# Retention's and attention's small steps placed on other tiles: value tile before root, last head one tile up, attention's products one tile back

## The reference, cut to what matters

```python
proj = h @ w_in                                   # block 1: q, k, v, g_ret, u, two gates
q = rope(q); k = rope(k) * 128 ** -0.5            # 8 heads of 128, v of 256 columns
scores = (q @ k.T) * decay ; inner = scores @ v   # causal, decay ** distance
ret = head_group_norm(inner + cross)              # (y - mean) * rsqrt(var + eps) per token
y_ret = (silu(g_ret) * ret) @ w_ret_out
y_s5 = ...                                        # 64 groups, complex diagonal scan, gelu, GLU
merged = sigmoid(gate_r) * y_ret + sigmoid(gate_s) * y_s5
x = x + gt_m * rmsnorm(merged @ w_out) ; x = x + gt_f * rmsnorm(ffn(x))
# block 2, one block of 256 keys: attention is causal softmax with ALiBi
p = softmax(q @ k.T * scale - slope * distance) ; o_a = p @ v
```

## Time and profile before

| | us |
|---|---|
| median of three runs (3452.05 to 3454.35) | 3454.16 |
| the profiled execution | 3456.49 |
| its span on the core | 3454.6 |
| PE busy | 3298.0 (95%) |
| DVE busy | 2389.5 (69%) |
| ACT busy | 1494.9 (43%) |

### The profile page before, as it was taken

How to read it: one execution, slowest core, us unless ns; L and a number is a source line. 1 busy time by engine, 2 the same in 40 slices (tenths; PEclk the granted TensorE clock), 3 DMA queues, 4 the chain that set the end, 5 groups by cost and what they waited for, 6 DMA issues and landing times.

```text
span 3454.6 us, 53480 instructions
## 1 busy us (share of the span) xinstructions
PE 3298.0 (95%) x20912; PEld 2990.6 (87%) x20912; DVE 2389.5 (69%) x2467; ACT 1494.9 (43%) x1538; POOL 445.8 (13%) x309
## 2 busy tenths in 40 slices
PE   1799999999989999999989999999999999999998
PEld 0799999999978888888868888888888888888887
DVE  8799987787676666655676667657767766666554
ACT  1455555544444344433354344344344444434332
POOL 2065556720100000000000000000002100000000
PEclk7899999999999999999999999999999999999999
DMA  9665554568745555567734444555555555555554
GB/s 399 269 235 219 217 206 173 187 246 302 300 151 184 194 186 190 190 233 258 266 111 167 171 159 175 191 182 190 193 183 198 185 190 187 193 185 190 190 190 146
DMA packets 111026, 706.34 MB, mean 204 GB/s; under 512 B 13376, under 2 KB 24256, under 8 KB 30672
## 3 DMA queue, kind: packets, MB, share of 16 engines
q1 hardware_dynamic: 100416, 693.86, 54.8%
q10 hardware_dynamic: 10512, 11.11, 1.0%
HBM read 702.83 MB, written 2.10 MB: 204 GB/s over the span
## 4 chain that ended last, share of the span: by engine, by line
PE 82%; DVE 8%; issue 4%; ACT 3%; POOL 2%; DMA 2%; DVEq 0%; ACTq 0%; POOLq 0%; SPq 0%
PE acc L523 44%; PE acc L524 23%; PE acc L520 4%; PE acc L521 4%; PE acc L522 4%; DVE ring_lo L1307 2%; ACT ring_hi L859 1%; DMA ring_raw<-w_ada 1%; DVE ring_raw L1329 1%; POOL s_w L1985 1%; PE p_norm L569 1%; POOL s_x L1987 0%; DVE aside_y L1329 0%; PE p_y L587 0%; POOL s_x L1984 0%
## 5 line engine op out<-in xcount | busy, mean ns | idle before, releaser
L1307 DVE TENSOR_TENSOR ring_lo<-ring_raw,ring_hi 128x2048 fp32r<-128x2048 f32 (+1 forms) x576 | 1312.4, 2280 | 571.8 <-ACT ring_hi L859 570.3
L523 PE MATMUL acc<-h_split,ring_hi 128*128 128x512 f32 x4736 | 1655.5, 392 | 9.2 <-DVE h_split L1369 4.5
L524 PE MATMUL acc<-h_split,ring_lo 128*128 128x256 f32 x4736 | 1337.5, 282 | 0.0
L859 ACT ACTIVATE ring_hi<-ring_raw 128x2048 fp32r<-128x2048 f32 (+1 forms) x576 | 1070.8, 1862 | 414.4 <-DMA ring_raw<-w_down 152.0
L523 PEld LDWEIGHTS acc<-h_split,ring_hi 128*128 128x128 f32 x4736 | 891.7, 188 | 197.3 <-issue 9.7
L524 PEld LDWEIGHTS acc<-h_split,ring_lo 128*128 128x128 f32 x4736 | 897.7, 190 | 0.4
L523 PE MATMUL acc<-ffn_split,ring_hi 128*128 128x512 f32 x1408 | 488.2, 390 | 0.0
L520 PE MATMUL acc<-h_split,ring_hi 128*128 128x256 f32 x1408 | 403.7, 287 | 82.9 <-DVE h_split L1369 69.8
L1926 POOL TENSOR_TENSOR sq_sum<-sq_sum,tile 128x256 f32<-128x256 f32 x60 | 76.6, 1277 | 2568.9 <-ACT tile L885 2568.9
L524 PE MATMUL acc<-ffn_split,ring_lo 128*128 128x256 f32 x1408 | 397.1, 282 | 0.0
L521 PE MATMUL acc<-h_split,ring_hi 128*128 128x256 f32 x1408 | 396.3, 281 | 0.0
(11 more groups left out here) (342 smaller groups left out, 3814.2 us busy)
## 6 DMA issues: line engine op xcount, KB each, us to landing
ring_raw<-w_ff SPq DMA_DIRECT2D x88, 1024.0 KB, 4.8
ring_raw<-w_down SPq DMA_DIRECT2D x64, 1024.0 KB, 4.8
ring_raw<-w_ffb SPq DMA_DIRECT2D x56, 1024.0 KB, 4.8
ring_raw<-w_heads SPq DMA_DIRECT2D x48, 1024.0 KB, 4.8
ring_raw<-w_mix SPq DMA_DIRECT2D x48, 1024.0 KB, 4.8
ring_raw<-w_ada SPq DMA_DIRECT2D x32, 1024.0 KB, 7.4
ring_raw<-w_ret SPq DMA_DIRECT2D x32, 1024.0 KB, 4.8
ring_raw<-w_glu SPq DMA_DIRECT2D x32, 1024.0 KB, 4.9
```

Source lines behind the costliest of these rows:

```text
L523: mm(dst[:], hi[s][:, t, :], moving[:, k, :], start=start, stop=False, skip_group_check=True)
L524: return mm(dst[:, T:], lo[s][:, t, :], moving[:, k, 0:T], start=False, stop=stop, skip_group_check=True)
L859: run(hi[s][:, 0:n, :], raw[s][:, 0:n, :], COPY).then_inc(hi_done, 1)
L1307: tt(lo[s][:, 0:n, :], raw[s][:, 0:n, :], hi[s][:, 0:n, :], SUB).then_inc(lo_done, 1)
```

## The change

Nothing is computed otherwise; instructions of PE, ACT and DVE stand at other places. In `heads`, ACT empties the bank of the second value tile ahead of the root, and DVE runs the S5 step ahead of the statistics at `r = 3` and `split_lo` ahead of the inverted root at `r = 4`. The last head's steps in `ret` move one tile up on all three engines: values after tile 0, statistics and root at tile 1, scaling and back-transposes at tile 2. In `att`, the transposes go from after `r = 1` to after `r = 2` and the value product from there to after the next head's `r = 0`, and ACT's and DVE's parts go along.

```diff
 # PE, phase ret
-                    if opening(g) and m in (1, 3):
-                        steps[3 * m // 2 + 1](ph["heads"].iters, 0, HEADS)
+                    if opening(g) and m in (0, 2):
+                        steps[3 * m // 2 + 2](ph["heads"].iters, 0, HEADS)
...
 # PE, phase att
-                        steps[r](g, i, 4 * g + i, (i + 1) % 2)
+                        if r == 0:
+                            if not (opening(g) and i == 1):
+                                att_values(g, i, n - 1, i % 2)
+                            att_scores(g, i, n, (i + 1) % 2)
+                        elif r == 2:
+                            att_turn(g, i, n, (i + 1) % 2)
...
 # PE, phase gla, tiles 0 to 5 of the first body
-                        if r < 3:
-                            att_rest[r](ph["att"].iters, 0, HEADS, 1)
+                        att_rest(r)       # 0: values of head 7, scores of 8; 2: turn; 3: values of 8
...
 # ACT, phase heads
-                        if r in (3, 4):
+                        if r == 4:
                             ret_step(r, g, i, n)
                     evac(p, g, m, m, (qk[:, 0, :], ..., v_t[:, 1, :], ...)[r])
-                    if r == 0 and not (opening(g) and i == 0):
+                    if r in (0, 3) and not (opening(g) and i == 0):
                         ret_step(r, g, i, n)
...
 # ACT, phase ret
-                    if opening(g) and m == 4:
+                    ahead(p, g, m)
+                    if opening(g) and m == 3:
                         ret_step(5, ph["heads"].iters, 0, HEADS)
-                    ahead(p, g, m)
                     s5_steps("ret", g, m, early=True, end=end)
-                    if opening(g) and m in (2, 3):
-                        ret_step(m + 1, ph["heads"].iters, 0, HEADS)
+                    if opening(g) and m == 2:
+                        ret_step(4, ph["heads"].iters, 0, HEADS)
                     if m < 4:
                         evac(p, g, m, m, m_ret[:, 4 * g + m, :], tanh=True)
+                        if opening(g) and m == 1:
+                            ret_step(3, ph["heads"].iters, 0, HEADS)
...
 # DVE, phase heads
-                    if prev[i] and r == 4:
-                        ret_before(r, g, i, n)
                     ahead(p, g, m)
-                    if prev[i] and r != 4:
+                    if prev[i] and r != 3:
                         ret_before(r, g, i, n)
                     s5_turned_back("heads", g, m)
+                    if prev[i] and r == 3:
+                        ret_before(r, g, i, n)
...
 # DVE, phase ret
-                    if opening(g) and m == 3:
+                    ahead(p, g, m)
+                    if opening(g) and m == 2:
                         ret_before(4, *last_head)
-                    elif opening(g) and m == 4:
+                    elif opening(g) and m == 3:
                         ret_out(HEADS)
+                    s5_turned_back("ret", g, m)
+                    if opening(g) and m == 1:
+                        ret_before(3, *last_head)
+                    elif opening(g) and m == 3:
                         ret_done(HEADS - 1, HEADS)
-                    ahead(p, g, m)
-                    s5_turned_back("ret", g, m)
-                    if opening(g) and m == 2:
-                        ret_before(3, *last_head)
...
 # ACT and DVE, phase att (and the same in gla): the copy of p_z at r == 2, DVE's division at r == 2,
 # and at r == 0, ahead of what they did there, for head n - 1:
+            def att_out(head, n):
+                act.wait_ge(A["summed"], n)
+                run(o_att[:, head, 0:T], p_o[:, 0:T], COPY).then_inc(A["hi"], 1)
+            def att_done(head, n):
+                dve.wait_ge(A["hi"], n)
+                done = o_att[:, head, :]
+                tt(done[:, T:], p_o[:, 0:T], done[:, 0:T], SUB).then_inc(A["done"], 1)
```

More of the change, by code:

```diff
@@ L753, in _ @@
                     i, r = divmod(m, 3)
+                    n = 4 * g + i
                     if not (opening(g) and m < 2):
@@ L761, in _, with att_rest @@
                         gate_up()
-            att_rest = steps
+            def att_rest(r):
+                if r == 0:
+                    att_values(ph["att"].iters, 0, HEADS - 1, 0)
+                    att_scores(ph["att"].iters, 0, HEADS, 1)
+                elif r == 2:
+                    att_turn(ph["att"].iters, 0, HEADS, 1)
+                elif r == 3:
+                    att_values(ph["att"].iters, 0, HEADS, 1)
             def gla_scores(g, i, n, par):
@@ L1192, in gate_end @@
                     ins.then_inc(B0["decays"], 1)
+            def att_out(head, n):
+                act.wait_ge(A["summed"], n)
+                run(o_att[:, head, 0:T], p_o[:, 0:T], COPY).then_inc(A["hi"], 1)
             def att_step(r, g, i, n):
                 if r == 0:
+                    if not (isinstance(n, int) and n == 1):
+                        att_out(4 * g + i - 2, n - 1)
                     act.wait_ge(A["turned"], n)
@@ L1258, in _ @@
                         att_step(r, ph["att"].iters, 0, HEADS)
+                    elif r == 3:
+                        att_out(HEADS - 1, HEADS)
             p = ph["conv"]
@@ L1732, in att_before @@
             def att_before(r, g, i, n):
-                if r == 1:
+                if r == 2:
                     dve.wait_ge(A["exp"], n)
@@ L1739, in att_before @@
                     ins.then_inc(A["p"], 1)
+            def att_done(head, n):
+                dve.wait_ge(A["hi"], n)
+                done = o_att[:, head, :]
+                tt(done[:, T:], p_o[:, 0:T], done[:, 0:T], SUB).then_inc(A["done"], 1)
             def att_after(r, g, i, n):
                 if r == 0:
+                    if not (isinstance(n, int) and n == 1):
+                        att_done(4 * g + i - 2, n - 1)
                     dve.wait_ge(A["scored"], n)
@@ L1748, in att_after @@
                     v.tensor_scalar(sm[:, 1, :], sm[:, 0, :], -QK_SCALE, None, MUL).then_inc(A["max"], 1)
-                elif r == 2:
-                    dve.wait_ge(A["hi"], n)
-                    done = o_att[:, 4 * g + i - 1, :]
-                    tt(done[:, T:], p_o[:, 0:T], done[:, 0:T], SUB).then_inc(A["done"], 1)
             p = ph["att"]
@@ L1828, in _ @@
                         att_after(r, ph["att"].iters, 0, HEADS)
+                    elif r == 3:
+                        att_done(HEADS - 1, HEADS)
                 own.leave(1 if isinstance(g, int) else p.iters - 1)
```

5 lines of the change are left out of this document (removed).

## The result

| | before | after |
|---|---|---|
| median, us | 3454.26 | 3470.44 |
| runs | 4 (3452.05 to 3456.05) | 4 (3469.41 to 3471.63) |
| ratio, 95% interval | | 1.0044 (1.003 to 1.0057) |
| profiled execution, us | 3456.49 | 3471.63 |
| its span, us | 3454.6 | 3469.6 |

The change makes the kernel 16 us slower, 15.1 between the two profiled executions. The forecast was 3468, inside a range of 3457 to 3477.

The account below looks back on a forecast made before the run. The prediction took a chain of DVE and ACT, not PE's stream, to set the heads' period. Heads +9.5, ret +8.0 and attention −3.7 made +13.8 us on the profiled 3456.49, so a median of 3468, range 3457 to 3477.

Parts of the forecast that it names:

- PE's wins at the bank: Heads, tile 11: 3.3 us of waiting become 1.7 for the low part and 3.1 for `o_t`; PE wins nothing.
- Second head: Heads, tiles 9 to 11: ACT's gelu step comes later, DVE's next splits with it; +0.95 us in each body.
- First head: Heads, tiles 3 to 5: later statistics delay high part and splits, S5 step starts late; +2.2 us in each of three bodies.
- PE's wait at tile 6: Heads: PE waits for `o_t` and the copy behind it before tile 6, some 4.4 us.
- all waits for `o_t`: Sign of being right: 25 to 32 us in about eight waits, three near 4.4, four of 1.5 to 3.1, one near 6.6.
- the low part at tile 11: Sign of being right, in the heads: PE waits about 1.6 us for `ring_lo` at tile 11.
- the heads' sum: Heads: three periods of 0.95 plus 2.2 us make +9.5 at the start of `ret`; bounds −16 and +24.
- Ret, +8.0: Last head in `ret`: PE waits 4 us for masked scores and 6.6 for `o_t`; +8.0 us, bounds 0 and +11.4.
- Attention, −3.7: Attention's transposes: shorter waits (−0.9 and −1.3) and half clock gone behind the first (−1.5); −3.7 us, bounds 0 and −7.0.
- Rival 1: Everything is covered: DVE's idle time in the heads swallows the later work and the waits go; 3434 us, chance 7%.
- rival 2: The heads come out even, DVE gives back its losses and only the order in `ret` costs; 3459.5 us, chance 15%.
- Rival 3: The clock decides: PE's longer waits in heads and `ret` bring half clock that shows in part; 3475.5 us, chance 16%.

Follow-up runs that it names:

- x_bank: Kernel before, with only ACT's copy of the second value tile out of its bank ahead of the root in the heads; 3456.12 against 3456.41 us.
- x_split: Kernel before, with the heads' value tile copied ahead of the root and DVE's weight split ahead of the inverted root; 3461.30 against 3457.07 us.
- x_s5: Kernel before, with the heads' value tile copied ahead of the root and the S5 step ahead of the statistics; 3456.97 us, ratio 1.0.
- x_heads: Kernel before, with only the change's part in the heads (value tile, S5 step, weight split); 3464.36 against 3456.41 us.
- x_ret: Kernel before, with only the last retention head's steps in ret one tile up; 3465.54 against 3456.41 us.
- x_root: Kernel before; in the heads ACT does value tile, decay factors, high part, then root; DVE splits ahead of the inverted root; 3456.82 against 3457.07 us.
- x_root2: Kernel before; heads' value tile and high part ahead of the root, decay factors behind it, DVE's split ahead of the inverted root; 3449.56 against 3455.38 us.
- x_att: Kernel before, with only attention's transposes and value products one tile back; 3453.31 against 3456.41 us.

## Why the prediction was right, point by point

- **PE's wins at the bank are lost again.** Right: x_bank takes away every one of them and is worth nothing. DVE and ACT's chain sets the period.
- **Second head, +0.95 a body.** Measured from the marks: the gelu handed over, +0.76, and statistics to gelu, 6.75 before and 6.85 after, +0.10: together +0.86. (x_split, with the bank's 0.4 us taken out, makes it 1.2.)
- **First head, +2.2 a body.** Measured from the first mark to tile 7: 34.80 before, 36.71 after, +1.9. That "both moves work together" is what x_s5 and x_split showed: the S5 step's move alone costs nothing. PE's wait at tile 6 was forecast at 4.4 us and is 3.44; all waits for `o_t` make 24.2 us in eight, just below the 25 to 32 in about eight that the prediction named. One sign that the prediction named is not there: PE does not wait for the low part at tile 11. It began that tile at 316.34 and the low part was out at 315.03, since half clock at tile 6 had made PE late too. That lateness costs nothing more: x_heads, with 6.8 us of half clock there, has the same period.
- **Where the heads' sum was off.** 86.12 to 88.81 is +2.7 a body in place of 3.15, and the three bodies together (from the transposes at 233.24 and 235.72 to those at 491.20 and 501.47) are 7.8 us longer in place of 9.5. But the first body's second head has the same steps, and the prediction counted three bodies only: from the first product to 233.24 before and 235.72 after it is 1.3 longer. With the 1.2 us of the start the mark at the end of the heads is 10.3 later. That the phase's +9.1 comes so near to the +9.5 is in part luck: three bodies were sized too high and a fourth was left out.
- **Ret, +8.0.** Measured +7.5, with the waits forecast at 4 and 6.6 us found at 3.66 and 5.86. x_ret alone gave +9.1, with 6 to 13 in its interval. The way there is not quite the forecast one. Tile 4, the first product of `ret_split`, began at 522.44 before and begins at 541.96 now: beyond the heads' 10.3 that is +9.3 in place of +8.1. The prediction has no term for half clock behind the wait for the scores (a granted clock of 0.50 from 512.6 to 515.9), and of the 9.3 some 1.7 us are given back by the mark in `glu`, where it expected nothing back.
- **Attention, −3.7.** Measured −3.0. The wait shrank to 2.35 us as forecast (2.4) and the last to 0.58 (0.9), but the half clock behind the first did not go. This is the term of the sum that failed. It was priced at −1.5 us and is not there: the granted clock is 0.52 behind the wait, near the 1.2 GHz level, against 0.50 before. The waits alone, forecast at −2.2, give −2.6. After:

```profile
1826.70:1830.20 3.50, 3.50 (x13) 3.02 (x12) 2.56 (x2) 3.18 (x10) 0.00 (x0) 0.52 0.42 176
```

Before:

```profile
1805.00:1808.40 3.40, 3.40 (x13) 2.92 (x12) 2.46 (x2) 3.40 (x9) 0.00 (x0) 0.50 0.00 0
```

- **Rival 1** (3434) and **rival 2** (3459.5) asked for a body no longer than before; it is 2.7 us longer. **Rival 3** (3475.5) had the facts of the clock right: half clock stood behind six of the seven waits for `o_t` in `heads` and cost PE about 1.5 us each time (in the window from 413.50 above, 16 matmuls in 3.4 us, where 0.118 us each make 1.9). It had the effect wrong, since DVE's marks do not move with it. Whether half clock is paid for in `ret` and `att` no run shows by itself.

The sum of +13.8 stands against a span that is 15.0 us longer, of which 1.2 lie ahead of the edits. That the rest is +13.8 as well is in part luck: the heads came out 0.4 below their term and `ret` 0.5 below, attention gave 0.7 less than forecast, and 0.2 more were lost between `glu` and attention.

What stays open is why the same unedited body of `ret` varies by 1.8 us between traces, and with it how exactly the loss in `ret` divides, and whether the 1.1 us between +15.1 (profiled) and +16.2 (medians) are more than the start: in all fourteen traces the first product comes between 106.1 and 110.6 us, and none of the edits stands ahead of it.

## What to carry to other kernels

When a stalled engine has the same period whether it is granted full or half clock, the stall is a symptom; look for the pair of engines that wait for each other, and measure the period between the same instruction of two iterations. Before moving a small step, ask what large step stands behind it on the other engine: here a root of 0.3 us held a high part of 1.9 and the split behind it. And a step that changes ACT's function carries its table load with it, so its neighbours must move along (x_root against x_root2: −0.3 and −5.8 us, the larger share of it the loads).

## What the hardware showed that was not expected

- **The place of half clock is not told by the length of a wait.** A wait of 3.2 to 3.3 us for the bank was followed by 1.00, by 3.4 us at 0.50 and by 6.8 us at 0.50, in the same kernel. In attention the wait of 3.3 us was followed by half clock before, and by full clock in x_bank, where it stood behind the later wait of 2.2 instead; the instructions of that phase are the same in both. Two windows of x_bank, behind these two waits:

```profile
1805.00:1808.40 3.40, 3.40 (x21) 3.03 (x22) 2.59 (x2) 3.40 (x11) 0.00 (x0) 1.00 0.20 82
1939.70:1943.10 3.40, 3.40 (x12) 2.81 (x12) 2.17 (x3) 1.61 (x1) 0.00 (x0) 0.51 0.25 106
```

  In the kernel after it stood behind waits of 1.7 us, in x_att behind one of 0.9. The Trainium skill, page "TensorE: Matmul & The Clock Gate", Part 1, has idle as the throttled default; these traces agree that half clock follows idle time, and show waits of 3.3 us without it.
- **Beside POOL the one that begins first keeps its time.** The same modulation row takes DVE 3.39 us before and 2.29 after the change, but working beside POOL is not what makes it slow. In the kernel before, the split at 358.47 began just ahead of a POOL operation and took its 2.28 us; that operation took 3.42 (another of the same shape, just ahead of it, 1.29) and still ran when the modulation row began at 360.67:

```profile
358.47 2.28 DVE L1307 TENSOR_TENSOR ring_lo<-ring_raw,ring_hi 128x2048 fp32r<-128x2048 f32 x1
358.49 3.42 POOL L1985 TENSOR_TENSOR s_w<-s_w,s_tab 128x512 f32<-128x512 f32 x1
```

  All 71 such operations of 128x2048 on DVE in the heads of this trace fit. The 44 that begin while no POOL operation runs take 2.26 to 2.29 us, also the 17 in which one begins meanwhile. The 27 that begin while one runs take 2.14 to 2.22 us plus what is left of it. With the S5 step moved, POOL's four operations behind it fall into DVE's wait for the high part. DVE is busy 2.6 us less in a body; what of that the period got no run shows.
